# Rotary position halves swapped by transfers within SBUF in place of a matrix product, in a two-block transformer kernel

## The reference, cut to what matters

```python
def rope(x, positions):
    d = x.shape[-1]
    half = d // 2
    inv_freq = jnp.power(ROPE_THETA, -2.0 * jnp.arange(half, dtype=jnp.float32) / d)
    ang = positions.astype(jnp.float32)[:, :, None, None] * inv_freq
    cos, sin = jnp.cos(ang), jnp.sin(ang)
    xf = x.astype(jnp.float32)
    x1, x2 = xf[..., :half], xf[..., half:]
    return jnp.concatenate([x1 * cos - x2 * sin, x1 * sin + x2 * cos], axis=-1).astype(x.dtype)
```

## Time and profile before

| | |
|---|---|
| three runs | 1750.53, 1754.97, 1756.06 us |
| median | 1754.97 us |
| the profiled execution | 1754.68 us, its span 1752.9 us |
| TensorE busy | 1696.5 us |
| VectorE busy | 1092.1 us |
| ScalarE busy | 745.3 us |
| GpSimd busy | 297.7 us |
| granted TensorE clock, mean | 0.991 |

### The profile page before, as it was taken

How to read it: one execution, slowest core, us unless ns; L and a number is a source line. 1 busy time by engine, 2 the same in 40 slices (tenths; PEclk the granted TensorE clock), 3 DMA queues, 4 the chain that set the end, 5 groups by cost and what they waited for, 6 DMA issues and landing times.

```text
span 1752.9 us, 32409 instructions
## 1 busy us (share of the span) xinstructions
PE 1696.5 (97%) x12781; PEld 1506.5 (86%) x12781; DVE 1092.1 (62%) x1748; ACT 745.3 (43%) x1111; POOL 297.7 (17%) x286
## 2 busy tenths in 40 slices
PE   5999999999999999999999999999999999999998
PEld 4776756788888888799999999999999999989986
DVE  6756476677664577865868664343753766654633
ACT  4367575365332342632323545447233643322323
POOL 2112197310000001532005221210102000000002
PEclk8999999999999999999999999999999999999999
DMA  9363542433333332264435752332543233332332
GB/s 313 101 151 97 157 120 73 144 88 102 99 96 98 94 96 75 70 180 126 129 105 145 232 145 83 96 122 75 170 116 97 71 87 95 92 100 85 96 94 75
DMA packets 321167, 201.18 MB, mean 115 GB/s; under 512 B 51279, under 2 KB 303814, under 8 KB 320918
## 3 DMA queue, kind: packets, MB, share of 16 engines
q1 hardware_dynamic: 300976, 160.79, 32.3%
q0 software_dynamic: 7952, 24.83, 4.7%
q10 hardware_dynamic: 12118, 13.88, 2.3%
HBM read 177.75 MB, written 17.24 MB: 111 GB/s over the span
## 4 chain that ended last, share of the span: by engine, by line
PE 83%; DVE 6%; ACT 4%; SPq 2%; issue 2%; DMA 1%; POOL 1%; ACTq 0%; DVEq 0%; POOLq 0%
PE ps L1467 69%; SPq L854 2%; DVE wlo L2153 1%; PE ps L1608 1%; PE ps L1768 1%; PE ps L1794 1%; PE ps L1778 1%; PE ps L1667 1%; PE ps L1998 1%; PE ps L1682 1%; PE ps L1584 1%; ACT whi L912 1%; DMA xrow<-in_x_dram 1%; PE ps L1924 0%; PE ps L1536 0%
## 5 line engine op out<-in xcount | busy, mean ns | idle before, releaser
L1467 PE MATMUL ps<-zhi,whi 128*128 128x258 f32 (+2 forms) x2072 | 639.3, 309 | 2.8 <-DVE wlo L2153 1.4
L1467 PE MATMUL ps<-zlo,whi 128*128 128x258 f32 (+2 forms) x2072 | 634.0, 306 | 0.0
L1467 PE MATMUL ps<-zhi,wlo 128*128 128x258 f32 (+2 forms) x2072 | 632.7, 305 | 0.0
L1467 PEld LDWEIGHTS ps<-zhi,whi 128*128 128x128 f32 x2072 | 391.2, 189 | 27.7 <-DVE wlo L2153 2.9
L2153 DVE TENSOR_TENSOR wlo<-stage,whi 128x1024 fp32r<-128x1024 f32 x256 | 322.7, 1262 | 139.0 <-ACT whi L912 127.0
L1467 PEld LDWEIGHTS ps<-zlo,whi 128*128 128x128 f32 x2072 | 390.5, 188 | 19.5 <-issue 1.0
L1467 PEld LDWEIGHTS ps<-zhi,wlo 128*128 128x128 f32 x2072 | 391.1, 189 | 18.2
L912 ACT ACTIVATE whi<-stage 128x1024 fp32r<-128x1024 f32 x256 | 269.4, 1055 | 314.8 <-PE ps L1467 260.3
L1467 PE MATMUL ps<-ghi,whi 128*128 128x512 f32 x340 | 134.7, 396 | 0.0
L1467 PE MATMUL ps<-glo,whi 128*128 128x512 f32 x340 | 134.2, 395 | 0.0
L1467 PE MATMUL ps<-ghi,wlo 128*128 128x512 f32 x340 | 134.0, 394 | 0.0
(11 more groups left out here) (426 smaller groups left out, 2836.2 us busy)
## 6 DMA issues: line engine op xcount, KB each, us to landing
stage<-in_w_up_dram SPq DMA_DIRECT2D x88, 512.0 KB, 3.8
stage<-in_w_in_dram SPq DMA_DIRECT2D x74, 512.0 KB, 4.0
stage<-in_w_down_dram SPq DMA_DIRECT2D x32, 512.0 KB, 4.0
ring<-in_w_ada_dram POOLq DMA_DIRECT2D x24, 512.0 KB, 4.4
adab<-in_w_ada_dram SPq DMA_DIRECT2D x16, 512.0 KB, 8.3
stage<-in_w_down_dram SPq DMA_DIRECT2D x16, 384.0 KB, 3.4
stage<-in_w_o_dram SPq DMA_DIRECT2D x8, 512.0 KB, 3.9
ring<-in_w_ada_dram SPq DMA_DIRECT2D x8, 512.0 KB, 3.8
```

Source lines behind the costliest of these rows:

```text
L1467: last = pe.matmul(out, w(a, k), x(k, t0, t1), start=(k == 0 and a is whi and x is x_hi), stop=(k == ks - 1 and a is wlo))
```

## The change

The matrices of the swap and their matmuls go away. Before GpSimd multiplies a piece by the cosine, it issues transfers that copy the two halves of every head, exchanged, from HT to rtp: 4 for each piece of groups 0 and 1 (32 partitions each) and 8 for each piece of group 2 (16 partitions each). GpSimd and VectorE then wait for the count of all transfers so far. VectorE's product with the sine reads rtp and writes it in place, one instruction for a piece in place of one for a tile. The sign is in the frequency constants, negative for the first half of a head: the sine changes its sign with it, the cosine does not. The semaphore gsin_done is now raised by VectorE's addition and no longer by its product, and the next piece's transfers wait for it, since there is one rtp. The load of ada piece 23 keeps its place behind the second piece.

```diff
-    def rot(w):
-        r = np.zeros((P, P))
...
-    misc[:, 0], misc[:, 1] = inv64, inv32
+    misc[:, 0], misc[:, 1] = np.where(p % 64 < 32, -inv64, inv64), np.where(p % 32 < 16, -inv32, inv32)
...
-    return np.concatenate([ident, ones, misc, b64, b32, rot(64), rot(32)] + mla + dil + [chunk],
+    return np.concatenate([ident, ones, misc, b64, b32] + mla + dil + [chunk],
...
+        TURN_DMAS = [P // (GROUPS[g]["w"] // 2) for g, _ in ROTS]
+        TURNS_IN = [16 * sum(TURN_DMAS[:i + 1]) for i in range(len(ROTS))]
+        JOB_OF = {t: job for job, (t, g, _) in RAW.items() if g >= 0}
...
-            def group_rot(g, p):
-                t0, n, _ = piece(g, p)
-                last = [J["dq"] + 3, J["dk"] + 3, J["qp"] + 1][g] if (g, p) != (2, 1) else J["kpe"]
-                wait_job_out(pe, last)
-                wait_job_out(pe, last - 1)
...
-                for m in range(n):
-                    mm = pe.matmul(ps[:, 1 + 2 * m, :], const("r%d" % GROUPS[g]["w"]), HT[:, t0 + m, :], start=True, stop=True)
-                mm.then_inc(grot_mm, 1)
...
             z1("dk", 0)
-            group_rot(0, 0)
             z1("dk", 1)
             group_stats(0)
-            group_rot(0, 1)
...
-                dve.wait_ge(grot_mm, i + 1)
+                dve.wait_ge(grot_in, TURNS_IN[i])
                 dve.wait_ge(tab_done, 1)
-                for m in range(n):
-                    ins = dve.tensor_tensor(rtp[:, m, :], ps[:, 1 + 2 * m, :], tab[:, w + 1, :], ALU.mult)
-                ins.then_inc(gsin_done, 1)
+                link(dve.tensor_tensor(rtp[:, 0:n, :], rtp[:, 0:n, :], tab[:, w + 1:w + 2, :].to_broadcast([P, n, T1]),
+                                       ALU.mult))
+                dve.wait_ge(gcos_done, i + 1)
+                dve.tensor_tensor(HT[:, t0:t0 + n, :], HT[:, t0:t0 + n, :], rtp[:, 0:n, :], ALU.add).then_inc(gsin_done, 1)
                 dve.wait_ge(gsin_done, i + 1)
-                dve.wait_ge(gcos_done, i + 1)
-                link(dve.tensor_tensor(HT[:, t0:t0 + n, :], HT[:, t0:t0 + n, :], rtp[:, 0:n, :], ALU.add))
...
+            def half_turn(g, p):
+
+                t0, n, _ = piece(g, p)
+                i, h = ROTS.index((g, p)), GROUPS[g]["w"] // 2
+                for t in range(t0, t0 + n):
+                    wait_job_out(pool, JOB_OF[t])
+                if i:
+                    pool.wait_ge(gsin_done, i)
+                for r in range(0, P, 2 * h):
+                    for d, f in ((r, r + h), (r + h, r)):
+                        pool.dma_start(rtp[d:d + h, 0:n, :], HT[f:f + h, t0:t0 + n, :]).then_inc(grot_in, 16)
+
             def cosines(g, p):
 
                 t0, n, w = piece(g, p)
-                pool.wait_ge(grot_mm, ROTS.index((g, p)) + 1)
+                pool.wait_ge(grot_in, TURNS_IN[ROTS.index((g, p))])
...
-            cosines(*ROTS[0])
-            cosines(*ROTS[1])
-            ada_load(pool, 23)
-            for g, p in ROTS[2:]:
+            pool.wait_ge(tab_ready, 2)
+            for i, (g, p) in enumerate(ROTS):
+                half_turn(g, p)
                 cosines(g, p)
+                if i == 1:
+                    ada_load(pool, 23)
```

More of the change, by code:

```diff
@@ L101, in host_constants @@
     misc[:, 64:] = p[:, None] // 16 == 2 * (p[None, :64] // 16)
-    return np.concatenate([ident, ones, misc, b64, b32, rot(64), rot(32)] + mla + dil + [chunk],
+    return np.concatenate([ident, ones, misc, b64, b32] + mla + dil + [chunk],
                           axis=1).astype(np.float32)
-CONST = {n: i * P for i, n in enumerate(["ident", "ones", "misc", "b64", "b32", "r64", "r32", "mla", "_m1",
+CONST = {n: i * P for i, n in enumerate(["ident", "ones", "misc", "b64", "b32", "mla", "_m1",
                                          "_m2", "_m3", "dil", "_d1", "_d2", "_d3", "chunk"])}
@@ L419, in emit @@
         lat_sum = sem("lat_sum")
-        grot_mm, gcos_done, gsin_done, ghead_done = (sem("grot_mm"), sem("gcos_done"),
+        grot_in, gcos_done, gsin_done, ghead_done = (sem("grot_in"), sem("gcos_done"),
                                                               sem("gsin_done"), sem("ghead_done"))
@@ L1728, in _ @@
             several("qp", 0, 4, lat)
-            group_rot(1, 0)
             group_stats(1)
             several("qp", 1, 4, lat)
-            group_rot(1, 1)
             z1("kpe", 0)
             several("kn", 0, 2, kvl)
-            group_rot(2, 0)
             several("kn", 1, 2, kvl)
@@ L1738, in _ @@
             several("kn", 2, 2, kvl)
-            group_rot(2, 1)
             several("kn", 3, 2, kvl)
```

## The result

The changed kernel took 1779.7 us, the median of 4 runs (1778.25 to 1781.33), against 1754.51 us for the kernel before in 4 runs beside it. The ratio is 1.0141, 95% interval 1.0129 to 1.0153: slower by 25 us, where 13.5 were forecast. 1779.7 is inside the range, near its upper end. The profiled execution took 1779.37 us (span 1777.5, which is 24.6 longer than the span before). The sine product and its addition are now lines 2320 and 2323, the group's scaling 2331, the transfers of a turn 2977, GpSimd's cosine product 2984; TensorE's plain matmul is line 1460.

The account below looks back on a forecast made before the run. TensorE's stream was taken to bound the kernel; after the change the serial chain of turns delays mv 0 by 11.9 us, the 9.5 us saved already inside. With 1.6 us of clock, 13.5 us slower: 1768 us, range 1757 to 1781.

Parts of the forecast that it names:

- the third rival: Turns' transfers land in 4.4 us, not 2.4, for four to six turns, 8 to 12 us more: 1777; chance 0.14.
- The bound and the chain of turns: Issue, landing, products, addition in series through rtp; group 2's scaling ends at 184.4 us, mv 0 starts 11.9 later.
- The 9.5 us of matmuls inside the waits: TensorE's 9.5 us of removed matmuls bring no further gain: it reaches its waits sooner and stands still.
- the first rival: Turns keep pace and TensorE's removed matmuls are won: gain 9.5 us or about half, 1745 to 1750; chance 0.08.
- The products exclude each other: In each turn GpSimd's 2.4 us and VectorE's 1.23 us product run one after the other, 3.7 us with semaphores.
- The second rival: Turns are late, but products overlap or landings are short: 1760, or 1757 with other short ends; chance 0.2.
- The issues: Each transfer's issue takes GpSimd 0.53 us: 2.1 us for a turn of four, 4.2 for eight.
- The clock: TensorE's granted clock falls after standstills between 177 and 195 us, adding 1.6 us once; ends 0 and 4.
- The landings: A turn's transfers from HT to rtp land in 2.4 us; ends 2.1 and 4.4.
- The late weights: The load waiting for unit 15's split lands 5.5 us late, TensorE stands about 2.5 us; doesn't add to turns' delay.
- From there on all is as before: After mv 0 starts, TensorE's work, ScalarE's last log and exp, and attention run as before; nothing absorbs the delay.

Follow-up runs that it names:

- the three-buffer versions: Changed kernel with three rtp buffers, transfers issued ahead: 1760.45 us from GpSimd's queue, 1759.44 with ada load 23 behind all turns, 1754.75 from SyncE's queue.
- with the loads held: Changed kernel, but SyncE holds weight load 16 until turn 2's transfers have landed and load 20 until turn 4's have: 1776.54 us, ratio 1.0113.
- the run with the split moved ahead: Changed kernel with VectorE's split of weight unit 15 moved from behind to ahead of turn 2's products: 1776.81 us, ratio 1.0125.
- the version with everything early: Changed kernel with three buffers, GpSimd's queue, turns 1 and 2 issued behind ada loads 20 and 21, ada load 23 last: 1752.97 us, ratio 0.9985.

## Why the prediction was right, and where it was short

That 1779.7 us lies inside 1757 to 1781 is owed to the width of the range. It is 1.3 us from the end, and nearer to the third rival's 1777, which had a chance of 0.14, than to the forecast of 1768. The direction and the chain of causes were right; one term of the sum was too small.

**The bound and the chain of turns: right.** Its two tests came out. TensorE is busy for 63.5 of the 85 us from 115 to 200, 21.5 less (20 to 25 forecast), and ScalarE's square waits for the scaling, 8.1 and 8.4 us (some 10 forecast). That the series through rtp is the cause, the three-buffer versions show.

**The 9.5 us of matmuls inside the waits: right**, by the run with the matmuls put back. Of the first rival (the turns keep pace) the lower price was the right one: 4 us, not 9.5, because ScalarE fills 150 to 170 us.

**The products exclude each other: right.** A turn took 4.8 us from landing to the end of the addition; 5.0 were forecast. In the five wide turns the delay showed on GpSimd's product (3.4 us) and not on VectorE's (1.23 us), where the prediction had looked for it; VectorE's started first, by some 0.05 us. The sum is the same. The Trainium skill ("SBUF — State Buffer", section on the two separate sides) says that such a pair excludes each other for the whole instruction. By that rule the trace agrees (3.40 us with VectorE's product ahead, 2.37 without). The second rival falls.

**The issues: right.** 484, 492 and 547 ns at the least, median and most; 530 forecast.

**The clock: right in size.** 1.6 us forecast, 1.5 measured. The prediction had it between 177 and 195 us. The clock was down there too, but the 1.5 us that cost time lie behind the start of mv 0 at 203.45.

**The landings: the step that failed.** The prediction said "I take 2.4, by the row that has the same size and both ends in SBUF". Forecast / measured, in us:

| turn | last issue to landing | addition done |
|---|---|---|
| 1 | 3.2 / 6.0 | 126.5 / 128.9 |
| 2 | 2.4 / 3.6 | 136.0 / 139.9 |
| 3 | 2.5 / 5.5 | 152.0 / 158.8 |
| 4 | 2.4 / 4.9 | 161.5 / 171.2 |
| 5 | 2.4 / 1.9 | 173.1 / 182.4 |
| 6 | 2.4 / 1.4 | 182.6 / 190.7 |

The landings sum to 23.3 us in place of 15.3, 8.0 more. Four times there are 0.6 us between the end of an addition and the next turn's first issue, 2.4 us, that the sum didn't have. The issues and products were 2.3 us shorter than taken; that these two nearly cancel is luck. Together 8.1: the scaling of group 2 ends at 192.5, not 184.4, and mv 0 at 203.45 in place of 195.3. Transfers by line, with the columns of the earlier trace rows:

```profile
rtp<-HT POOLq DMA_DIRECT2D x16, 128.0 KB, 4.8
...
rtp<-HT POOLq DMA_DIRECT2D x8, 64.0 KB, 2.4
...
rtp<-HT POOLq DMA_DIRECT2D x8, 32.0 KB, 1.8
```

The 2.4 us were right for transfers that no load is issued among: 2.3 to 2.4 in turns 2 and 4 with the loads held. What was missed is that one event starts both. VectorE's addition releases GpSimd's issues, the split right behind it on VectorE (128.91) frees a weight buffer, and SyncE issues its load 0.7 us behind the turn's first transfer. Turns 2 and 4 met these loads and took 1.2 and 2.5 us more than forecast. Turns 1 and 3 took 2.8 and 3.0 more. The prediction had seen that GpSimd's ada load stands right ahead of them (115.53 and 145.97), but had priced it too low, and SyncE's loads were issued beside them as well (from 117.17 and from 141.17). Moving the ada load away took 1.8 us off turn 3; turn 1's landing no run isolates. The third rival (long landings, 1777) had the right size, but for it the prediction named only those ada loads, and against it that turns 4 to 6 meet few loads. Turn 5, whose SyncE load was issued 0.2 us behind its last issue (175.85), and turn 6, without any, have smaller transfers and were quicker than forecast.

The Trainium skill ("DMA: Bandwidth & Descriptors", section on the anatomy of one DMA) gives a fixed 2.0 us and the bytes at 436 GB/s. For 128 KB that makes an estimate of 2.3 us. By the profile's own measure, from the issue itself to the landing, the turns with the loads held come near it (the row is turn 2's; turn 4's median is the same), and the 4.8 of the changed kernel doesn't:

```profile
rtp<-HT POOLq DMA_DIRECT2D x4, 128.0 KB, 2.7
```

**The late weights: nearly right.** The load of unit 17 was forecast 5.5 us late, with TensorE standing for 2.5 us; it was issued 9.4 us late (141.17), and TensorE stood for 4.31 us, up to 149.01. The late weights were said not to add; the run with the split moved ahead allows some 2 us.

**"From there on all is as before": nearly.** After the clock's term the shift is 21.6 us, yet the span is 24.6 longer. 2.2 us of it come at one place in the recurrence stage. TensorE waits 1.95 us for ScalarE there, before 1.36, and then works at a lower granted clock (0.87 from 1050 to 1060 us; before, 1.00 from 1030 to 1040). The same ten matmuls, first in the changed kernel, then before:

```profile
1057.15 2.01 PE L2002 MATMUL ps<-QH,KH 128*128 128x128 f32 x10 [0.65 <-DVE sT L2859]
```

```profile
1034.96 1.26 PE L2028 MATMUL ps<-QH,KH 128*128 128x128 f32 x10 [0.65 <-DVE sT L2886]
```

This doesn't follow the turns: at the same place the shift against the kernel before doesn't grow in the profiled run with the split moved ahead (21.3 us ahead of it, 21.2 behind), and grows by 3.9 us in the one with the matmuls put back. The last 0.9 us, at the end of the span, come in the run without transfers as well; their cause stays open.

So of 11.7 us missing in the forecast (25.2 against 13.5), 8.1 are in the turns (8.0 of landings and 2.4 of gaps, less the 2.3), about 3 lie far behind them, in the recurrence stage and at the end, and the rest lies between medians and single spans.

## What to carry to other kernels

In this kernel a transfer within SBUF in place of an engine's operation paid (by some 0.15%) only where it was issued a landing ahead of its use, which took a buffer per turn in flight, and a place in the queue where its source is just ready. Behind its predecessor's consumer it added issue, landing and semaphore to every step. When you cost a landing, list what the same event releases on the other queues, and take the price from a row with such a load beside it. And before counting on removed work of the bounding engine, look at who comes second: here ScalarE left 4 of 9.5 us.

## What the runs showed of the hardware that was not expected

- Four transfers of 128 KB within SBUF landed between 1.7 and 6.6 us after the last issue in the versions with one buffer, by what else was in flight. With no load issued among them it was 1.7 from SyncE's queue (turns 2 and 4, one with a 512 KB load right ahead in the same queue, the other with one right behind) and 2.3 to 2.4 from GpSimd's. With a SyncE load among them it was 3.6 to 5.6, and with GpSimd's ada load among them (turn 3 in SyncE's queue) 6.0. In turns 1 and 3, with GpSimd's 512 KB load right ahead and SyncE's loads beside them, it was 5.4 to 6.6. Holding a load back by 4 us gave turns 2 and 4 1.3 and 2.6 us.
- From the end of VectorE's addition to GpSimd's first issue there are 0.6 us, in all four turns whose issues wait for nothing else.
- TensorE's busy total hardly fell, from 1696.5 to 1695.9 us, though 9.5 us of matmuls were gone. In the version with everything early, which issues the same 12759 matmuls, it is 1684.8. The 11 us lie where the granted clock is lower. The same 495 matmuls, up to the first attention scores, are busy for 104.42 us in the changed kernel (110 to 237.86 us, granted clock 0.92) and for 95.43 us in the other (110.52 to 211.95 us, 1.00), and those of the place in the recurrence stage for 17.40 us (0.91) and 15.71 us (1.00). I put the difference down to the clock. About 3 us of it (1.5 behind the start of mv 0, 1.6 at 1057 us) came out as time, the rest lay beside waits: a busy total of TensorE doesn't say how much work it has.
